# The second group's w_out, query and projection matmuls cut into parts that stand among the dot products

## The reference

```python
def peer_ffn(h, w_q, keys1, keys2, u_tab, v_tab):
    q = (hf @ w_q).reshape(tokens, PEER_HEADS, 2, PEER_HALF)
    s1 = jnp.einsum('thd,hnd->thn', q[:, :, 0], keys1)
    s2 = jnp.einsum('thd,hnd->thn', q[:, :, 1], keys2)
    v1, i1 = lax.top_k(s1, PEER_TOPK); v2, i2 = lax.top_k(s2, PEER_TOPK)
    ...
    top_score, pos = lax.top_k(cand_score, PEER_TOPK)     # 16 experts of 8 heads: 128 per token
    gate = jax.nn.softmax(top_score, axis=-1)
    ...
        act = jax.nn.gelu(jnp.einsum('tkd,td->tk', u_tab[idb], xb))
        return jnp.einsum('tk,tkd->td', gb * act, v_tab[idb])
```

## Time and profile before

| | |
|---|---|
| median of 3 runs | 1753.78 us (1751.03 to 1754.48) |
| the profiled execution | 1757.92 us |
| its span, first to last instruction | 1756.2 us |
| PE busy | 1280.1 us (73%) |
| DVE busy | 1123.6 us (64%) |
| POOL busy | 985.1 us (56%) |
| ACT busy | 249.9 us (14%) |
| mean DMA rate over the span | 341 GB/s |
| moved by the gathers (software queue) | 536.94 MB |
| moved by SyncE's loads and stores | 61.42 MB |
| mean granted TensorE clock | 0.844 of full |

### The profile page before, as it was taken

One profiled execution on the slowest core, in us unless ns is written; L12 is line 12 of the kernel. 1 busy time (PEld: TensorE's weight loads), 2 busy tenths in 40 slices (PEclk: granted clock), 3 DMA queues, 4 the chain that ended last, 5 costly groups with the idle time before them and its releaser, 6 DMA issues.

```text
span 1756.2 us, 18406 instructions
## 1 busy us (share of the span) xinstructions
PE 1280.1 (73%) x5996; PEld 676.7 (39%) x5996; DVE 1123.6 (64%) x2951; ACT 249.9 (14%) x479; POOL 985.1 (56%) x1067
## 2 busy tenths in 40 slices
PE   7999899987687967769758755554796565557666
PEld 6898569844355544546314400110271001001011
DVE  4623259686677887776846676678756677766440
ACT  3322321212232321010101000000010000000000
POOL 3000006455666646455657767776777677777764
PEclk9999899998898988587878968887798767876889
DMA  4222618889999999798999999999999999999998
GB/s 147 93 92 83 249 27 329 326 346 406 360 385 371 410 387 370 281 332 302 400 403 409 409 399 391 410 410 409 410 409 409 358 409 410 409 410 409 409 369 308
DMA packets 160081, 599.53 MB, mean 341 GB/s; under 512 B 19057, under 2 KB 19057, under 8 KB 154353
## 3 DMA queue, kind: packets, MB, share of 16 engines
q0 software_dynamic: 147456, 536.94, 78.4%
q1 hardware_dynamic: 12528, 61.42, 8.9%
HBM read 596.18 MB, written 2.10 MB: 341 GB/s over the span
## 4 chain that ended last, share of the span: by engine, by line
PE 29%; DMA 23%; DVE 17%; POOL 17%; issue 10%; DVEq 3%; ACT 1%; ACTq 0%; POOLq 0%; SPq 0%
DMA arena<-in_peer_v,arena 15%; POOL arena L554 9%; POOL arena L543 8%; DMA arena<-in_peer_u,arena 8%; PE psum L848 6%; DVE arena L1449 5%; PE psum L812 5%; PE psum L594 4%; PE psum L796 2%; PE psum L592 2%; PE psum L712 1%; PE psum L705 1%; DVE arena L1139 1%; PE psum L695 1%; DVE arena L1349 1%
## 5 line engine op out<-in xcount | busy, mean ns | idle before, releaser
L848 PE MATMUL psum<-arena 128*32 128x512 f32 x2048 | 595.0, 791 | 333.8 <-DMA arena<-in_peer_v,arena 277.5
L1449 DVE CUSTOM_DVE_ANT_0 arena<-arena,psum 128x1024 f32<-128x1024 f32 x512 | 613.9, 1218 | 309.7 <-DMA arena<-in_peer_u,arena 302.3
L543 POOL DMA_INDIRECT arena<-in_peer_u,arena x512 | 483.9, 945 | 433.1 <-PE psum L796 244.2
L554 POOL DMA_INDIRECT arena<-in_peer_v,arena x512 | 484.1, 946 | 322.6 <-PE psum L848 187.3
L848 PEld LDWEIGHTS psum<-arena 128*32 128x32 f32 x2048 | 99.4, 127 | 783.1 <-DMA arena<-in_peer_v,arena 574.0
L812 PEld LDWEIGHTS psum<-arena 128*128 128x128 f32 x1024 | 116.2, 193 | 9.2 <-issue 9.2
L594 PE MATMUL psum<-arena 128*128 128x256 f32 x512 | 118.3, 386 | 1.7 <-DMA arena<-in_w_in 1.6
L812 PE MATMUL psum<-arena 128*128 128x128 f32 x1024 | 118.1, 276 | 1.6 <-ACT arena L1021 1.6
L594 PEld LDWEIGHTS psum<-arena 128*128 128x128 f32 x512 | 96.4, 193 | 21.8 <-issue 9.1
L592 PE MATMUL psum<-arena 128*128 128x256 f32 x384 | 90.6, 394 | 5.3 <-DVE st L1181 4.1
L592 PEld LDWEIGHTS psum<-arena 128*128 128x128 f32 x384 | 74.4, 197 | 21.0 <-DVE st L1181 4.5
(11 more groups left out here) (216 smaller groups left out, 1257.2 us busy)
## 6 DMA issues: line engine op xcount, KB each, us to landing
arena<-in_w_in SPq DMA_DIRECT2D x28, 1024.0 KB, 7.0
arena<-in_peer_w_q SPq DMA_DIRECT2D x16, 1024.0 KB, 15.2
arena<-in_w_out SPq DMA_DIRECT2D x16, 512.0 KB, 6.9
arena<-in_peer_u,arena POOLq DMA_INDIRECT x512, 10.1
arena<-in_peer_v,arena POOLq DMA_INDIRECT x512, 10.1
arena<-in_x SPq DMA_DIRECT2D x4, 512.0 KB, 4.1
out<-arena SPq DMA_DIRECT2D x16, 128.0 KB, 5.6
arena<-in_norm_g SPq DMA_DIRECT2D x1, 512.0 KB, 18.1
```

What stands on the lines that cost most here:

```text
L543: pool.indirect_dma_start(u_row[n % UB], None, u_d, bass.IndirectOffsetOnAxis(ap=eid[i % 2][:, c:c + 1], axis=0)).then_inc(u_in[n % UB], 16)
L554: pool.indirect_dma_start(v_row[n % VB], None, v_d, bass.IndirectOffsetOnAxis(ap=eidT[k % (2 * PH // UH)][:, at_:at_ + 1], axis=0)).then_i ...
L848: mm = pe.matmul(bank[6 + half][group * UK:(group + 1) * UK], zrows[k % 2][:, z0:z0 + ZW], v_row[n % VB][:, half * 512:(half + 1) * 512], ...
L1449: dve.tensor_tensor_reduce(u_row[n % UB], u_row[n % UB], h2p, 1.0, 0.0, ALU.mult, ALU.add, dots[:, c:c + 1]).then_inc(s["u_free"], 1)
```

## The change

The steps `wo` and `q` of the second group are cut into four parts each, its `proj` into two. In the table of places each part has an equal share of its step's cost, so it lands at an n of its own where the costs allow. The first part carries TensorE's waits, the last part keeps the step's own name. ACT, DVE and SyncE act on that name alone: they follow the last part. PSUM banks are given out as before.

```diff
+IN_PARTS = {"wo": 4, "q": 4, "proj": 2}
+
+
+def parts_of(step):
+    kind, t, i = step
+    return [(kind + str(k), t, i) for k in range(IN_PARTS.get(kind, 1) - 1)] + [step]
...
-    steps = second_group()
+    steps = [(part, c / len(parts_of(step))) for step, c in second_group() for part in parts_of(step)]
...
     for j, step in enumerate(route(2)):
-        at.setdefault(END + 9 + 3 * j, []).append(step)
+        for k, part in enumerate(parts_of(step)):
+            at.setdefault(END + 9 + 3 * j + min(k, 2), []).append(part)
...
     for j, step in enumerate(route(3)):
-        at.setdefault(2 * SEL + 86 + 2 * j, []).append(step)
+        for k, part in enumerate(parts_of(step)):
+            at.setdefault(2 * SEL + 86 + 2 * j + k // 2, []).append(part)
...
+                if chunks[-1] == DC - 1:
+                    mm.then_inc(filled("proj", g, u)[0], 1)
...
+                    chunks = share(DC)
+                    if chunks[0] == 0:
+                        claim("wo", t, i)
+                        for a in range(2):
+                            pe.wait_ge(*read("mix", t, a))
...
+                    for c in chunks:
                         mm = pe.matmul(ps, mixT[t][:, c], w_out_s[t // GT][c][:, i * 512:(i + 1) * 512], start=c == 0, stop=c == DC - 1)
-                    mm.then_inc(filled("wo", t, i)[0], 1)
+                    if chunks[-1] == DC - 1:
+                        mm.then_inc(filled("wo", t, i)[0], 1)
```

More of the change, by code:

```diff
@@ L184, with whole @@
 SCALE_AT, BEGIN, END = 18, 20, 207
+IN_PARTS = {"wo": 4, "q": 4, "proj": 2}
+def parts_of(step):
+    kind, t, i = step
+    return [(kind + str(k), t, i) for k in range(IN_PARTS.get(kind, 1) - 1)] + [step]
+def whole(step):
+    kind, t, i = step
+    if kind[-1].isdigit() and kind[:-1] in IN_PARTS:
+        return (kind[:-1], t, i), int(kind[-1])
+    return step, IN_PARTS.get(kind, 1) - 1
 def places():
     at = {}
-    steps = second_group()
+    steps = [(part, c / len(parts_of(step))) for step, c in second_group() for part in parts_of(step)]
     at.setdefault(SCALE_AT, []).append(("xsc", 1, 0))
@@ L240, in layer_kernel @@
     USE, filled_so_far, turn = {}, [0] * 8, 0
-    for step in ORDER:
+    for part in ORDER:
+        step, k = whole(part)
+        if step + (0,) in USE:
+            continue
         got = banks_of(step, turn)
@@ L579, in claim, with project @@
                 return bank[b]
-            def project(g, u):
+            def project(g, u, chunks):
                 name, part, k = unit(g, u)
                 slot, b = u // 2 % WRING[g], u // 2
[L584 to L588, removed]
+                if chunks[0] == 0:
+                    claim("proj", g, u)
+                    if k == 0:
+                        pe.wait_ge(w_block_in[g][slot], 16 * (b // WRING[g] + 1))
+                ps, w = bank_for("proj", g, u), wbuf[g][slot]
+                for dc in chunks:
                     if u == 0:
@@ L594, in project @@
                         mm = pe.matmul(ps[:, 0:WCOLS], hT[g][:, dc, k * P:(k + 1) * P], w[:, dc], start=dc == 0, stop=dc == DC - 1)
-                mm.then_inc(filled("proj", g, u)[0], 1)
+                if chunks[-1] == DC - 1:
+                    mm.then_inc(filled("proj", g, u)[0], 1)
             def gate_steps(g, i):
@@ L749, in delta, with step_, share @@
                     mm.then_inc(filled("os", t, 0, 1)[0], 1)
-            def step_(kind, t, i):
+            def step_(*step):
+                (kind, t, i), part = whole(step)
+                in_parts = step[0] != kind or step not in BEFORE
+                def share(n):
+                    m = IN_PARTS[kind]
+                    return range(part * n // m, (part + 1) * n // m) if in_parts else range(n)
                 if kind == "ht":
@@ L758, in step_ @@
                 elif kind == "proj":
-                    project(t, i)
+                    project(t, i, share(DC))
                 elif kind == "ga":
@@ L804, in step_ @@
                 elif kind == "q":
[L805 to L810, removed]
+                    some = share(4)
+                    if some[0] == 0:
+                        claim("q", t, i)
+                        if i == 0:
+                            pe.wait_ge(s["wq_in"], 16 * DC * (t // GT + 1))
+                            for a in range(2):
+                                pe.wait_ge(*read("h2T", t, a))
+                    ps = bank_for("q", t, i)
+                    for j in some:
                         for c in range(DC):
-                            mm = pe.matmul(ps[:, j % 4 * P:(j % 4 + 1) * P], w_q_s[t // GT][c][:, j * HALF:(j + 1) * HALF], h2T[:, c],
-                                           start=c == 0, stop=c == DC - 1)
-                    mm.then_inc(filled("q", t, i)[0], 1)
+                            mm = pe.matmul(ps[:, j * P:(j + 1) * P], w_q_s[t // GT][c][:, (4 * i + j) * HALF:(4 * i + j + 1) * HALF],
+                                           h2T[:, c], start=c == 0, stop=c == DC - 1)
+                    if some[-1] == 3:
+                        mm.then_inc(filled("q", t, i)[0], 1)
                 elif kind == "s":
```

10 lines of the change are left out of this document (4 added, 6 removed).

## The result

The changed kernel takes 1757.63 us (median of 11 runs, 1751.77 to 1766.0), the kernel before 1751.95 us (median of 11 runs on the same chip, 1749.8 to 1756.75). The ratio is 1.0033, with a 95% interval of 1.0017 to 1.0049: slower by 3.0 to 8.6 us, and by more than the 0.2% that a measurement can tell. The profiled execution took 1759.09 us (span 1757.4), 1.2 us more than that of before; but that one stood some 6 us above its median and this one 1.5, so the two traces lie closer together than the medians do. Each kernel has one trace, so a difference of 2 us in one stretch can be chance.

A forecast was written before the change was run, and what follows sets the result against it. DMA transfers were taken to bound the phase, with gains only at their pauses. +3.0 at units 22 and 23 and -1.8 at `wo` of tile 2 gave +1.2 us: median 1755.0 us, range 1746.0 to 1764.0.

The forecast's parts named there:

- The likeliest case: Whole kernel: time within 3.5 us of before, around 1755.0 us; chance 0.43.
- What bounds it: Whole phase: the DMA transfers at about 409 GB/s bound it, so an edit gains only where they pause.
- Units 6 to 19: Second halves of projection units 6, 9, 12, 16, 19: rows up to 1.8 us earlier, costed at nothing.
- The convolution moved behind `weigh(3)`: Unit 22's convolution, before v104: moves behind L1435, taking 2.4 us from the path to the rows at 131.
- The loads move out of the stall: POOL's stall before v104: 3.67 MB of `w_in` and `w_out` loads start 13 us later, with the returning gathers.
- the first place: Units 22 and 23, around the stall before v104: +3.0 us, ends -2.4 and +9.0.
- The inverse does not live on the transfers alone: Triangular inverse, n = 141 to 191: runs at 289 GB/s, an argument against paying the unfilled stall in full.
- `wo` of tile 2: Rows at 183 and 187: 3.5 and 1.8 us earlier, taken as -1.8 us, ends 0 and -4.0.
- `wo` of tile 3 and the queries: Rows at 199, 203, 223 and 227: shifts covered by full-rate transfers, nothing taken; uncovered, up to 6 and 3 us.
- the paid stall: Late loads before the inverse never regained: +9.0 us at most, 1761 to 1763 us; chance 0.22.
- the second place: `wo` of tile 2, rows at 183 and 187: forecast to gain 1.8 us.
- The clock: TensorE's clock falls after idling, so parts with short waits slow it, in queries 5 us or more; slower chance 0.09.

## Why the prediction was right or wrong

The time came inside the range (1757.6 of 1746.0 to 1764.0), on the slower side that had a chance of 0.31. The likeliest case, no change to tell, was wrong: +1.2 us was forecast, +5.7 measured. The profiled execution was forecast at 1759.1 us and took 1759.09; that is luck. A term sized at +3.0 came to +10.6, and -3.3, -2.0 and -1.95 us in stretches that stood at nothing, the last before the change begins, brought the sum back.

- **What bounds it**: right. All that changed, but for 2 us before v96, lies at the DMA's pauses between 610 and 850 us; the stretch at 408 GB/s stayed at 405, and v160 to v448 changed by 0.3 us.
- **Units 6 to 19, "nothing"**: -1.97 us from v0 to v96. One pair of traces can't tell this from chance, and the cost of nothing may stand. If it is real, rows that come up to half a unit earlier did help. The traces of the other chips lean the same way (334.4 us on average with the projection in parts, 341.1 without), but differ by up to 22 us among themselves.
- **The convolution moved behind `weigh(3)`, -2.4**: right in kind. POOL's stall is 16.16 us (about 16 was forecast), and v96 to v104 takes 1.63 us less.
- **The loads move out of the stall**: right, 650.52 for a forecast near 653, and the DMA pauses from 640 to 650.
- **The price of it, +3.0 us at the first place: this is the term that failed.** From v96 to v120 it is -1.63 + 12.20 = +10.6 us, beyond the upper end of +9.0. Two steps of its working were wrong. It let the loads fill the weak stretches behind the stall. They stayed weak: counted from the issue of v104, 167 and 324 GB/s, before 215 and 338, though POOL issued without a pause and the loads left 2.0 us behind v104. (Where they left with v104, in the late-load runs, they did fill them.) And the sum ended at dot product 141, forecast at 674.8 and seen at 676.73, as if nothing came behind it. The rows at 139 waited for v107 until 672.91, they hold the buffers of v112, and POOL, which had waited for nothing there, waited 7.50 us; so the pause went on to the next gathers, and v120 still waited 7.86. I had named v107 ("near 672") and not asked which gather its rows release. (The sum for it counts eight gathers; v107 is the seventh from v104 on, which makes it 671 by the same rate. The rows used it at 672.91.)
- **"The inverse does not live on the transfers alone"**: right, and too weak an argument. It gave back 3.34 us from v120 to v152, which I had not counted, out of 12.20.
- **`wo` of tile 2, -1.8**: right in this pair of traces, and not shown beyond it. v156 no longer waits, and v152 to v160 is 1.71 us shorter, but v160 waits 2.17 us where it waited 1.33, and on the other chips there is no gain.
- **`wo` of tile 3 and the queries, nothing**: right on the first chip (+0.24 us), with v172 at 1.24 us of wait (under 2 forecast) and v200 at 2.87 (about 1 forecast). The rows at 227 come later, as forecast, at 965.91 for 961.40. That they cost nothing holds by the cover alone: where TensorE gets its matmuls one by one, the same order costs 8.2 us.
- **The rivals**: the paid stall is what came. Its sign was that "u141 lands over 3.5 us later than now, plus the 1.8 that the second place gives back", which is 5.3; it is 4.65 later in the trace's own time, 6.6 counted from v0 and 8.6 from v96, just ahead of this place. By the last two my own sign of being wrong, over 5 us, has come as well. The other, the stretch from n = 141 to 191 by more than 3 us, has not: dot products 141 to 191 take 169.1 us, before 170.5. Its price of +9.0, or +7.2 with `wo` of tile 2, is a little above the +5.7 measured; the 3.34 us that came back in the inverse would make up for it. The clock played no part on the first chip that I can show: from 690 to 775 us it is 0.68 in both traces. The rule that bursts cut by waits fall back to the slow clock (the Trainium skill, "TensorE: Matmul & The Clock Gate", section "HAM oscillation — how this bites in real kernels") agrees with the trace as to the clock: while TensorE waited for v107 its granted clock fell to 0.50, the lower of its two levels (670 to 675 us), and the rows took 3.29 us for ten records, where in the earlier trace rows all sixteen took 1.92. That wait was the transfers' doing, not a cut between parts.

What is shown and what is not: that the loads left the stall, that u138 to u141 and v106, v107 landed late and that v112 then waited is shown by the trace of the first chip. That this alone makes the 5.7 us is my reading of it. The experiment made for it, late loads without parts, cost nothing in the total in any of five runs, on chips where ScalarE's unexplained waits set the stretch behind the stall, and with loads that leave 2 us earlier than in the change. Up to v112, where these waits can be left out, it cost 1.4 to 2.6 us of the 7.2 that the first chip shows. Whether late loads alone cost some 5 us on the first chip stays open, and so does the share of the parts themselves there.

## What to carry to other kernels

A stall of one engine is not always lost: look at what else runs in it. Here 9 us of loads did, set off by an instruction that stood before the wait, and placing half of that instruction's work behind the wait took them along. When transfers are made late, follow them through the buffer ring: ask which consumer gets its row late, which gather that consumer releases, and go on until a gather waits no longer than before. The first late arrival (forecast at +2.7 us here) is only the start of the bill. And a burst before a ring's consumer should be short enough to survive a slow moment: one and a half queries between two rows cost nothing on the first chip and 8 us where TensorE got its matmuls one by one. Last, an experiment that moves one thing should move it to the same place: loads that left with the first gather filled the restart of the DMA, and loads that left two microseconds behind it did not.

## What the hardware showed that I had not expected

The same kernel takes 1752 us on one chip and 1932 to 1953 us on others (five chips, 17 to 35 executions on each), and the difference is not the rate of the DMA, which is about 410 GB/s there too while gathers are under way. It is idle time before instructions for which the profile names no releaser. Who waited for whom, in the changed kernel on the first chip, the largest of TensorE and of VectorE (total us, times, longest):

```profile
PE psum L860 <- issue: 2.2, 3, 0.7
...
DVE arena L1489 <- issue: 5.1, 12, 1.3
```

And on the last chip:

```profile
PE psum L888 <- issue: 72.6, 51, 17.4
...
DVE arena L1489 <- issue: 57.1, 48, 4.8
```

All such waits together are 2.2 us on TensorE, 12.9 on VectorE and 0.3 on ScalarE on the first chip, 177, 172 and 772 us on the last (ScalarE is idle most of the time on both, so its sum says least); the spans are 1757.4 and 1924.7 us. In the stretch of the queries shown above they come as one instruction every 1.4 to 2.1 us for 10 us, while the DMA is full (406 to 410 GB/s from 1015 to 1040 us); the longest of TensorE's is 17.4 us. What feeds the engines so slowly there no run shows. Two consequences do show: what a part of the change costs depends on the chip (queries in parts change v192 to v240 by 0.03 us on the first chip and by 8.2 us on the others), and the mean rate of the transfers falls from 340 to 311 GB/s although they run at about 410 while gathers are under way.

The restart after a pause was the other surprise. With gathers issued every 1.2 us and 3.67 MB of loads sent 2.0 us behind the first of them, the DMA took 10 us from v104 on to come to its full rate (167, 324, then 411 GB/s in steps of 5 us); without loads beside them it took as long (215, 338, 404 in the kernel before). Only where the loads left with the first gather was it full after 5 us (279, then 417). Why that is so no run shows.
